# A half unit's split issued ahead of, instead of behind, each step of other work on ScalarE, VectorE and GpSimd

## The chip, the cores and the metric

The kernel runs on one core of a Trainium2 chip. The metric is the device time of one execution in microseconds (us). TensorE, VectorE, ScalarE and GpSimd appear in the profile as PE (weight loads apart as PEld), DVE, ACT and POOL; SyncE is SP.

## What is computed

The reference is a network of ten stages on one batch of 256 tokens of width 1024, all in float32. The first block has two layers. Layer 0 is a chunked gated linear attention with a small memory attention; layer 1 is a stick-breaking attention with the same kind of memory attention; each is followed by a PEER layer, which scores 2 x 128 keys for each of 8 heads, takes the best 16 of each side, then the best 16 of the 256 sums, and applies the chosen experts out of 16384:

```python
def peer(x, w_q, subkeys, u_tab, v_tab):
    ...
    s = jnp.einsum('nhpd,hpkd->nhpk', q, subkeys).astype(jnp.float32)
    top_s, top_i = lax.top_k(s, PEER_TOPK)
    ...
    best_s, best_pos = lax.top_k(cand_s, PEER_TOPK)
    idx = jnp.take_along_axis(cand_i, best_pos, axis=-1)
    g = jax.nn.softmax(best_s, axis=-1).astype(x.dtype)
    ...
        act = jax.nn.gelu(jnp.einsum('nd,nhkd->nhk', xt, u_tab[it]), approximate=False)
        return jnp.einsum('nhk,nhkd->nd', gt * act, v_tab[it])
```

The second block has two layers of feed-forward, mixer, feed-forward. The mixer joins four attentions (neighbourhood `na`, differential `df`, grouped `gq`, dilated `dl`) between one input and one output projection. All weights together are 933 units of 128 x 1024 numbers, and every unit is read once.

## The kernel before, in words

**Units and halves.** SP loads each unit (512 KB) into one of four buffers `RAW` (line 2542). A unit is used as two halves of 128 x 512. TensorE does not take float32 at full precision here: every weight half is split into a high part `WH` (ScalarE, `Scalar.split`, line 1026, the activation at line 1037) and a low part `WL` = `RAW` - `WH` (`Vector.split`, line 1573, at line 1580; for every fourth half of most stretches GpSimd instead, `Gpsimd.split`, line 2302, at line 2309; `low_on_pool` at line 32 says which). Both have `NHALF` = 5 slots. Each product is then three matmuls: high by high, high by low, low by high. All of TensorE's matmuls are recorded at line 415 and its transposes at line 419.

**What a split waits for.** `Scalar.split` of half j waits until its `RAW` has landed and until TensorE has used half j - 5, whose slot it takes over. The low split waits for the high one. TensorE waits, ahead of half j, for its low part. SP waits for both low parts of a unit before it loads the buffer again.

**The order of work.** The four engines run four programs that walk the same list of halves. TensorE does half j, then a `tick()`. On the other three, `halves(n)` does per half: a `tick()`, then the split of the half five ahead. At the start five halves are split, so when TensorE does half j, the other engines do `tick()` j and then the split of half j + 5. `Pace.tick` (line 99) advances every generator in `fg` by one step and those in `bg` by as many steps as the stage's `rate` gives credit for; each step yields its cost, the same number on each engine, so that step k of a generator lies at the same half on all four. The steps are the "other work": the attention of each kind (scores, turn, values), the norm and rotation of queries and keys (`norm`), the linear attention (`decay`, `inner`, `states`), the stick-breaking heads (`two_heads`), and in a PEER stage `route` and `gates`. Every engine takes its instructions in the order written.

**Around the ticks.** Work outside `tick()` stands between calls of `halves`: the copies out of PSUM after a group of halves, `gelu` on ScalarE after each pair of `u` units (line 1399), the split of the gate activations `GH` (ScalarE, line 1374) and `GL` (VectorE, line 2100) ahead of each `v` unit, and the norms between stages. At a stage's end four halves are held back and used together (`last_two`), and `next_stage` splits four halves with no tick between them.

**The PEER stage** (`peer_stage`: 851, 1376, 2102, 2431) has 32 halves of query projection; 128 halves of `u` with `route` in the background (rate 3.5, both blocks of 128 tokens, one after the other); 128 halves of `u` with `gates` part 0 (rate 0.55); then 256 halves of `v`, the first 128 of them with `gates` part 1. `route` on VectorE is a search for the top 16 (lines 1966 to 1987) and then a decode of wide operations (lines 2008 to 2046); GpSimd has two multiplications of it (line 2420). At its end TensorE transposes the result, for which it waits on the last of VectorE's reductions (line 2045). A step of `gates` is on VectorE either two comparisons (lines 2078, 2081) or three products and one multiplication out of PSUM (lines 2086, 2093), and in every second step TensorE does 24 small matmuls. In the first 128 halves of `v` GpSimd has no splits. For the `v` unit g TensorE waits for `GL` of g; there are two buffers of it, so `GL` of g + 1 is made while TensorE works on g.

**The stages without steps.** The feed-forward stages have no background work. Those with `which` = 1 have `mix_tables`: on ScalarE five loads at the first tick and one small exponential at the last, on GpSimd from the 13th tick some scalings and sums, on VectorE five small operations at the last.

Of the kernel before, what the change touches and what calls it, by code (L numbers as in the profile page):

```python
# [1017 lines left out]
class Scalar:  # L1018
# [20 lines left out]
    def halves(self, n):  # L1039
        for _ in range(n):  # L1040
            self.j += 1
            self.pace.tick()
            self.split()

    def start_load(self, name, dst, src):
        sem, n = self.c.load(name)
# [519 lines left out]
class Vector:  # L1566
# [14 lines left out]

    def halves(self, n):
        for _ in range(n):
            self.pace.tick()
            self.split()

    def own(self):

# [706 lines left out]
class Gpsimd:  # L2295
# [14 lines left out]

    def halves(self, n):
        for _ in range(n):
            self.pace.tick()
            self.split()

    def next_stage(self, stage):
        self.e.wait_ge(*self.c.xtl.at(stage + 1, 1, 1))
# [424 lines left out]
```

## Time and profile before

| | |
|---|---|
| median of 3 runs | 3193.7 us (3188.42 to 3195.05) |
| the profiled execution: its own time | 3195.57 us |
| its span in the trace | 3193.5 us |
| busy: PE, DVE, ACT, POOL | 95%, 66%, 50%, 15% |
| granted TensorE clock, mean | 0.974 |
| chain that ended last | PE 85%, DVE 10%, ACT 3%, issue 1%, DMA 1% |

The busy shares say which engine has work; the waits of PE, stage by stage, say what keeps it from working. A wait stands in brackets behind the instruction that ended it: `[2.60 <-DVE BIG L1767]` is 2.60 us in which the engine was idle, ended by VectorE's instruction at line 1767. The stages begin at about 75 (rest of the linear attention's projections), 174 (PEER), 1036 (stick-breaking), 1175 (PEER), 2042, 2244 (mixer), 2421, 2620, 2821 (mixer) and 2998 us of the span.

### The profile page before, as it was taken

Reading aid. Unit: us, or ns where it says so; the run is one execution under the profiler, and the core shown is the slowest. Engines: PE = TensorE matmul, PEld = TensorE weight load, DVE = VectorE, ACT = ScalarE, POOL = GpSimd, SP = SyncE. Lnnn points to the kernel's source line nnn. Section 1 sums busy time; section 2 is a strip of 40 time slices with the busy share of each in tenths; the row PEclk is TensorE's granted clock in tenths of the full one; section 3 lists DMA queues with packets and bytes.
Section 4 is the critical chain, followed back from the end, with each engine's and each line's share of the span. In section 5 each row is a group of like instructions: output and inputs, shape, how many; then the busy total and the mean of one; then the engine's idle time right before and its main releaser. Section 6 shows DMA issues by size and latency. Waiting matters only on the chain.

```text
span 3193.5 us, 56060 instructions
## 1 busy us (share of the span) xinstructions
PE 3029.3 (95%) x21820; PEld 2730.7 (86%) x21820; DVE 2097.6 (66%) x4342; ACT 1597.0 (50%) x3039; POOL 492.8 (15%) x371
## 2 busy tenths in 40 slices
PE   8989999999998989999999999799979999998899
PEld 8789999988787879999988888699768989976798
DVE  4559988799655456987879945654665455456544
ACT  5445544444555545554444455455535555553454
POOL 1213210000021112320000022222101213210121
PEclk9999999999999999999999999899989999999999
DMA  6345554444554334554445555455314556542354
GB/s 213 119 146 170 180 166 159 160 161 164 187 192 160 127 122 160 171 173 158 159 159 166 166 198 195 171 187 180 126 59 149 190 181 197 185 141 70 113 188 155
DMA packets 139512, 512.60 MB, mean 161 GB/s; under 512 B 15713, under 2 KB 16242, under 8 KB 137970
## 3 DMA queue, kind: packets, MB, share of 16 engines
q1 hardware_dynamic: 134352, 489.22, 46.6%
q10 hardware_dynamic: 4898, 19.81, 1.7%
q8 instruction: 174, 2.85, 0.4%
q14 instruction: 88, 0.72, 0.1%
HBM read 507.92 MB, written 1.05 MB: 159 GB/s over the span
## 4 chain that ended last, share of the span: by engine, by line
PE 85%; DVE 10%; ACT 3%; issue 1%; DMA 1%; ACTq 0%; DVEq 0%; SPq 0%
PE ps L415 84%; DVE WL L1580 2%; ACT WH L1037 1%; PE ps L419 1%; ACT BIG L1133 1%; DVE BIG L1692 1%; DVE BIG L1741 1%; DMA RAW<-in_w 0%; DVE XTl L1619 0%; DVE BIG L1655 0%; DVE H L1658 0%; DVE BIG L2025 0%; DVE BIG L1986 0%; DVE BIG L2032 0%; DVE BIG L1633 0%
## 5 line engine op out<-in xcount | busy, mean ns | idle before, releaser
L1037 ACT ACTIVATE WH<-RAW 128x512 fp32r<-128x512 f32 x1866 | 1168.5, 630 | 1193.8 <-PE ps L415 1167.1
L1580 DVE TENSOR_TENSOR WL<-RAW,WH 128x512 fp32r<-128x512 f32 x1537 | 1109.7, 725 | 868.6 <-ACT WH L1037 860.7
L415 PE MATMUL ps<-XTh,WH 128*128 128x256 f32 x3928 | 1131.6, 288 | 22.4 <-DVE XTl L1788 8.2
L415 PE MATMUL ps<-XTl,WH 128*128 128x256 f32 x3928 | 1120.6, 285 | 0.0
L415 PE MATMUL ps<-XTh,WL 128*128 128x256 f32 x3928 | 1119.9, 285 | 0.0
L2309 POOL TENSOR_TENSOR WL<-RAW,WH 128x512 fp32r<-128x512 f32 x329 | 441.3, 1341 | 2652.8 <-ACT WH L1037 2652.8
L415 PEld LDWEIGHTS ps<-XTh,WH 128*128 128x128 f32 x3928 | 762.9, 194 | 34.1 <-DVE WL L1580 14.5
L415 PEld LDWEIGHTS ps<-XTl,WH 128*128 128x128 f32 x3928 | 763.5, 194 | 3.1
L415 PEld LDWEIGHTS ps<-XTh,WL 128*128 128x128 f32 x3928 | 762.8, 194 | 0.0
L415 PE MATMUL ps<-WH,GH 128*128 128x512 f32 x1408 | 562.5, 399 | 20.0 <-DVE GL L2100 8.1
L415 PE MATMUL ps<-WL,GH 128*128 128x512 f32 x1408 | 554.0, 393 | 0.0
L415 PE MATMUL ps<-WH,GL 128*128 128x512 f32 x1408 | 553.2, 393 | 0.0
L415 PEld LDWEIGHTS ps<-WH,GH 128*128 128x128 f32 x1408 | 267.3, 190 | 78.1 <-issue 9.8
L415 PEld LDWEIGHTS ps<-WH,GL 128*128 128x128 f32 x1408 | 267.0, 190 | 57.8
L415 PEld LDWEIGHTS ps<-WL,GH 128*128 128x128 f32 x1408 | 267.6, 190 | 50.2
L415 PE MATMUL ps<-BIG 128*128 128x64 f32 (+6 forms) x966 | 154.2, 312 | 23.7 <-DVE BIG L1769 5.8
L415 PEld LDWEIGHTS ps<-BIG 128*128 128x128 f32 (+4 forms) x966 | 124.1, 190 | 48.5 <-issue 22.8
L415 PE MATMUL ps<-WH,XTh 128*128 128x512 f32 (+1 forms) x400 | 158.0, 395 | 4.4 <-DVE XTl L1619 1.3
L415 PE MATMUL ps<-WH,XTl 128*128 128x512 f32 (+1 forms) x400 | 150.1, 375 | 0.0
L415 PE MATMUL ps<-WL,XTh 128*128 128x512 f32 (+1 forms) x400 | 149.9, 375 | 0.0
L419 PE MATMUL ps<-CST,BIG 128*128 128x128 f32 x430 | 78.4, 322 | 61.7 <-DVE BIG L1692 36.6
L419 PEld LDWEIGHTS ps<-CST,BIG 128*128 128x128 f32 x430 | 59.8, 166 | 83.1 <-DVE BIG L1692 41.6
(182 smaller groups left out, 2209.3 us busy)
## 6 DMA issues: line engine op xcount, KB each, us to landing
RAW<-in_w SPq DMA_DIRECT2D x933, 512.0 KB, 3.3
BIG<-in_ln ACTq DMA_DIRECT2D x4, 1024.0 KB, 6.3
GAIN<-in_norms ACTq DMA_DIRECT2D x6, 512.0 KB, 4.1
BIG<-in_sk ACTq DMA_DIRECT2D x2, 1024.0 KB, 5.0
BIG<-in_na_bias ACTq DMA_DIRECT2D x2, 1024.0 KB, 10.2
BIG<-in_qk_gain ACTq DMA_DIRECT2D x2, 960.0 KB, 6.6
BIG<-in_memT ACTq DMA_DIRECT2D x4, 256.0 KB, 7.6
BIG<-in_xT ACTq DMA_DIRECT2D x1, 1024.0 KB, 5.5
```

What stands on the lines that cost most here:

```text
L415: return self.e.matmul(out, lhsT, rhs, start=start, stop=stop, skip_group_check=loose)
L419: return self.e.transpose(out, in_, self.c.IDENT[0:n, 0:n])
L1037: e.activation(wh, raw, ACT.Copy).then_inc(*c.hi.mark(j))
L1133: e.activation(t.E[:, i % 3, w], src[:, w], ACT.Exp, bias=s[:, blk:blk + 1], accum_out=s[:, 2 + blk:3 + blk]).then_inc(*c.exps.mark(tag, i ...
L1580: e.tensor_tensor(wl, raw, wh.bitcast(F32), ALU.subtract).then_inc(*c.lo_v.mark(j))
L1692: e.scalar_tensor_tensor(out=c.XN[:, blk, w], in0=c.H[:, blk, w], scalar=s[:, 3:4], in1=c.GAIN[:, w], op0=ALU.mult, op1=ALU.mult).then_inc ...
L1741: e.tensor_reduce(s[:, 0:2], src, AX, ALU.max, negate=True).then_inc(*c.maxed.mark(tag, i))
L2309: e.tensor_tensor(wl, raw, wh.bitcast(F32), ALU.subtract).then_inc(*c.lo_p.mark(j))
```

## The change

In the three programs that split, `halves` calls `self.split()` ahead of `self.pace.tick()`. The program of TensorE and that of SP are untouched, and so are `next_stage`, the start and all that stands between calls of `halves`. No instruction is added or removed.

```diff
@@ Scalar
     def halves(self, n):
         for _ in range(n):
             self.j += 1
+            self.split()
             self.pace.tick()
-            self.split()
@@ Vector
     def halves(self, n):
         for _ in range(n):
+            self.split()
             self.pace.tick()
-            self.split()
@@ Gpsimd
     def halves(self, n):
         for _ in range(n):
+            self.split()
             self.pace.tick()
-            self.split()
```

## Rows read from the trace of the kernel before

**Rows 1.** The page's first part: busy time, share of the span, instructions.

```profile
PE 3029.3 (95%) x21820; PEld 2730.7 (86%) x21820; DVE 2097.6 (66%) x4342; ACT 1597.0 (50%) x3039; POOL 492.8 (15%) x371
```

**Rows 2.** Waits of PE in the whole span: us in total, times, longest.

```profile
PE ps L415 <- DVE WL L1580: 8.0, 14, 2.5
PE ps L415 <- POOL WL L2309: 5.4, 2, 2.7
```

**Rows 3.** Groups by form: instruction xcount | busy, mean ns | idle before, releasers.

```profile
L1037 ACT ACTIVATE WH<-RAW 128x512 fp32r<-128x512 f32 x1866 | 1168.5, 630 | 1193.8 <-PE ps L415 1167.1 <-DMA RAW<-in_w 8.6 <-DVE XTl L1619 6.8
L1580 DVE TENSOR_TENSOR WL<-RAW,WH 128x512 fp32r<-128x512 f32 x1537 | 1109.7, 725 | 868.6 <-ACT WH L1037 860.7
```

**Rows 4.** Chain that ended last, behind the first route block: start, us, what.

```profile
322.88 59.04 PE ps L415 x492
```

**Rows 5.** Timeline of DVE in the first route block: start, us, instruction, idle before.

```profile
290.46 0.69 DVE L1580 TENSOR_TENSOR WL<-RAW,WH 128x512 fp32r<-128x512 f32 x1 [0.60 <-ACT WH L1037]
...
303.98 3.40 DVE L2032 TENSOR_TENSOR BIG<-BIG,CST 128x1024 f32<-128x1024 f32 x1
...
321.07 1.20 DVE L2045 TENSOR_REDUCE BIG<-BIG 128x64 f32<-128x1024 f32 x1
```

**Rows 6.** Timeline of POOL in the same block.

```profile
303.54 2.76 POOL L2420 TENSOR_TENSOR BIG<-BIG 128x1024 f32<-128x1024 f32 x1 [1.77 <-DVE BIG L2025]
306.26 3.94 POOL L2309 TENSOR_TENSOR WL<-RAW,WH 128x512 fp32r<-128x512 f32 x2
```

**Rows 7.** Timeline of PE in the same block: its two waits.

```profile
308.55 0.39 PE L415 MATMUL ps<-XTh,WH 128*128 128x256 f32 x1 [2.68 <-POOL WL L2309]
...
322.33 0.55 PE L419 MATMUL ps<-CST,BIG 128*128 128x128 f32 x3 [0.53 <-DVE BIG L2045]
```

**Rows 8.** Windows behind the first wait: PE, PEld, DVE, ACT, POOL busy, clock, DMA, GB/s.

```profile
309.80:313.10 3.30, 3.30 (x18) 3.30 (x17) 3.30 (x4) 0.66 (x2) 0.40 (x1) 0.50 0.49 158
```

**Rows 9.** Timeline of ACT among the first `v` units, with gates.

```profile
650.27 0.63 ACT L1037 ACTIVATE WH<-RAW 128x512 fp32r<-128x512 f32 x1 [0.79 <-PE ps L415]
```

**Rows 10.** Timeline of DVE there.

```profile
651.06 0.69 DVE L1580 TENSOR_TENSOR WL<-RAW,WH 128x512 fp32r<-128x512 f32 x1
651.66 0.42 DVE L2100 TENSOR_TENSOR GL<-BIG,GH 128x256 fp32r<-128x256 f32 x1
...
652.84 1.09 DVE L2086 TENSOR_TENSOR OHW<-ROWS,GT 128x512 bf16<-128x512 bf16 x3
653.85 0.68 DVE L2093 TENSOR_TENSOR BIG<-BIG,ps 128x512 f32<-128x512 f32 x1
```

**Rows 11.** Timeline of PE there: a half of six matmuls, then the gate matmuls.

```profile
651.37 0.39 PE L415 MATMUL ps<-WH,GH 128*128 128x512 f32 x1
...
652.73 0.90 PE L415 MATMUL ps<-ROWS,GAIN 128*128 128x64 bf16 x24
653.47 0.48 PE L415 MATMUL ps<-WH,GH 128*128 128x512 f32 x1
```

**Rows 12.** Timeline of ACT in the first mixer stage.

```profile
2327.82 0.63 ACT L1037 ACTIVATE WH<-RAW 128x512 fp32r<-128x512 f32 x1
```

**Rows 13.** Timeline of DVE there.

```profile
2328.48 0.69 DVE L1580 TENSOR_TENSOR WL<-RAW,WH 128x512 fp32r<-128x512 f32 x1 [1.07 <-ACT WH L1037]
2329.09 0.35 DVE L2171 TENSOR_TENSOR BIG<-BIG 128x192 f32<-128x192 f32 x1
```

**Rows 14.** Timeline of PE there, with the first and last such wait.

```profile
2271.42 1.14 PE L415 MATMUL ps<-BIG 64*128 64x256 f32 x8 [0.59 <-ACT BIG L1506]
...
2328.64 0.60 PE L419 MATMUL ps<-CST,BIG 128*128 128x128 f32 x4
...
2331.84 1.08 PE L415 MATMUL ps<-BIG 128*128 128x64 f32 x8 [2.60 <-DVE BIG L1767]
...
2396.42 1.08 PE L415 MATMUL ps<-BIG 128*128 128x64 f32 x8 [0.55 <-DVE BIG L1769]
```

**Rows 15.** Waits of PE from 1036 to 1175, the stick-breaking stage; columns as in rows 2.

```profile
PE ps L415 <- DVE BIG L1943: 2.0, 2, 1.2
```

## The prediction

> **What bounds the kernel now.** I read the page first, then PE's waits, the groups by form, the chain, and the timelines of five places. TensorE is busy 95% of the span [rows 1], so only what reaches its waits can move the time. A whole one: what is earlier or later on another engine, and is not waited for, is worth nothing. The splits are the largest work of ScalarE and VectorE, but both sit idle ahead of them: ScalarE 1167.1 us until TensorE has used a half, VectorE 860.7 us until ScalarE has the high part [rows 3]. TensorE waits the other way, for a low part, only 8.0 us in 14 times on VectorE and 5.4 us in 2 times on GpSimd [rows 2]: 13.4 us is all that an earlier split can give directly. The five halves of lead hide the rest.
>
> **What the change does to the order.** No instruction is added, so no duration changes by itself. On each engine the old order is step j - 1, split j + 4, step j, split j + 5; the new one is split j + 4, step j - 1, split j + 5, step j. Between two steps there stands one split, before and after. What differs is which: step j now stands behind split j + 5, which needs TensorE's half j to be done, where it stood behind split j + 4, which needed half j - 1. So a step that could begin while TensorE was in half j now waits for its end, then for ScalarE's split and, on VectorE, for its own. Only where a step of ScalarE is itself late, beyond the end of half j, is nothing lost. In return each low part is ready earlier by the step that stood before it.
>
> Moved with the steps are the five loads of `mix_tables` (ScalarE's queue, behind one split of 0.63 us; used twelve ticks later: nothing). SP's queue is not reordered; its waits are on low parts, which come no later relative to TensorE in the quiet stages, and earlier in the busy ones. In the projections of the feed-forward and in the last 128 halves of `v` the steps are empty: nothing.
>
> **Route, four blocks (two layers, two blocks of tokens).** Here both effects meet. In the decode, GpSimd multiplies from 303.54 for 2.76 us and only then does its split, from 306.26 [rows 6]; TensorE waits 2.68 us for that low part [rows 7], and behind the wait its clock is granted at 0.50 for 3.3 us [rows 8]: half of that, some 1.6 us, is lost as well. The new order does this split ahead of the multiplication, so both should go: 4.3 us a block, 17 in four. But VectorE has no gap between its split at 290.46 and the reduction at 321.07 over 0.2 us [rows 5], and TensorE, at 322.33, waits for that reduction, if only 0.53 us [rows 7]. VectorE sets when the block ends, so TensorE arrives earlier and waits there instead. And VectorE enters the full stretch later. At 290.46 it had finished its step and was idle 0.60 us [rows 5]; now it has the split first and the step behind it, so all later steps come one step and 0.6 us of idle time later. A step of the search is some 0.8 us: TensorE's half lasts 1.44 us (59.04 us for 492 matmuls, twelve to a half [rows 4]), less some 0.6 for the split. Together +1.4 us. The idle time of TensorE at the reduction becomes 0.5 + 4.3 + 1.4, some 6 us in one piece, and 2.68 us was enough to bring the clock down [rows 7, 8]; what it costs behind the reduction, 1.6 us, is not covered any more, as nothing follows on which TensorE would have waited. Bounds of a block: 0 (VectorE has reserves that I don't see) and +3.0. I take +2.0, nearer the upper one since the stretch is full. Four blocks: **+8**.
>
> The multiplication also holds up VectorE: L2032, begun 0.44 us after it, took 3.40 us [rows 5, 6]. "SBUF — State Buffer" of the Trainium skill (Who interferes with whom) says that an elementwise operation of VectorE with two inputs in SBUF and a GpSimd operation exclude each other, the later one blocked until the first is done; the row agrees. By that rule a GpSimd split moved ahead only changes which operation of VectorE stands still, and the sum stays.
>
> **First 128 halves of `v`, two stages.** GpSimd has no splits there and VectorE is nearly full. A half is 1.36 us and the gate matmuls add 0.74 [rows 11]. `GL` of the next unit must be there when TensorE ends its two halves. Old: at 650.27 ScalarE begins the split [rows 9], some 0.1 us after the half's end; VectorE's split follows at 651.06, `GL` at 651.66 [rows 10], 1.4 us after ScalarE's start. New: the step stands between split and `GL`. For the long kind it is 1.6 us (from 652.84 to 0.6 us behind 653.85 [rows 10]). From the half's end: 0.74 to the high part, 0.6 split, 1.6 step, 0.42 `GL` makes 3.36 us; TensorE needs it at 0.74 + 2 x 1.36 = 3.46. It fits by 0.1 us, and misses by about 0.1 where a short step ran just before. Taken: ten misses a stage, +1 us each stage. Bounds: 0, and +12 a stage if each of the 32 long steps costs a further 0.4 (the 0.42 of `GL` come free of cover). Two stages: **+2**.
>
> **Mixers, two stages.** Between 2271.42 and 2396.42 TensorE waits 17 times for steps, from 0.2 to 3.5 us; the first, one of the longest and the last have a row [rows 14]. In the wait at 2331.84 the chain is: ScalarE's split at 2327.82 [rows 12], VectorE's at 2328.48, its rotation from 2329.09 [rows 13], then L1767, then TensorE. In the new order this split is that of the half that TensorE ends at about 2328.6, where its transposes begin [rows 14]: ScalarE starts at about 2328.65 and not at 2327.82, so the wait is longer by 0.8 us. Where ScalarE was late itself, with exponentials beyond the half's end, it costs nothing. Bounds for a stage: 0, and 17 x 0.8 = 14. I take five of the 17, four microseconds, nearer the lower end since in most of them the attention's own chain goes on through the end of the half. Two stages: **+8**.
>
> **Stick-breaking.** Twelve heads, with TensorE waiting 2.0 us in 2 times for VectorE's mask [rows 15], so this chain has just run out of reserve; each of the six pairs can lose up to the 0.8 us of above. Bounds 0 and +5; taken **+3**.
>
> **Linear attention and start.** In the four `tokens` steps ScalarE's copy now stands behind a split of 0.63 us [rows 3], and the last of them leads into the next stage: +0.6. The steps of `decay`, `inner` and `states` are chains of several engines: bounds -1 and +4, taken +1.4. Together **+2**.
>
> **Sum:** 8 + 2 + 8 + 3 + 2 = +23 us on the profiled execution of 3195.57 us (span 3193.5), so 3218.6. That execution is 1.9 us above the median of the three, 3193.7; the forecast against the median is **3217 us**, 0.7% slower. What this measurement can tell from no change is about 0.2%, 6.4 us.
>
> A rule speaks against the change in one sentence: "ScalarE/VectorE/GpSimdE queues are strict FIFO" ("PSUM — Partial Sum Buffer" of the Trainium skill, Engine vs sequencer instructions). By it a waiting split holds all steps behind it; that VectorE's rotation starts at the end of the split, with 1.07 us idle before it [rows 13], agrees.
>
> **Rivals.** (a) *The starved splits were the cost* (faster). TensorE no longer waits in the decode, and VectorE ends the reduction early enough because the reordered GpSimd work holds it up less (3.40 us for one operation [rows 5] shows how much there is to win). It decides if VectorE reaches the reduction more than 0.5 us earlier than now. Then up to 4.3 us a block come back, -17, and with the mixers at 0 the time is 3177. For it: it is the only place with waits for low parts of over 2 us. Against: the unbroken row of work of VectorE. 0.12.
>
> (b) *Hidden.* Steps lose their head start, but PE's next demand lies two steps later almost everywhere; the mixers' chains are bound by ScalarE. Then 3194 to 3200. For it: 95% busy. Against: the wait at 2331.84. 0.12.
>
> (c) *`GL` becomes the bound* (slower by more). The 0.1 us of reserve above is not there; 12 us for each stage on top, and the upper halves of mixers and stick-breaking: 23 + 22 + 8 = +53, 3245. 0.14.
>
> That the change does nothing would need the waits of a split never to bite; it is in (b), since for the empty stages it is true.
>
> **How the numbers follow.** The forecast has 0.62; it lies over 6.4 us in 0.57 of it. Faster: 0.11 of (a). Same: 0.01 of (a), 0.12 of (b), 0.05 of the forecast: 0.18. Slower: 0.57 and the 0.14 of (c): 0.71. The range leaves out most of (a) and the upper half of (c): 3190 to 3242. Lower end: everything at its lower bound but a few us back in the decode; upper end: route 12, `v` 12, mixers 16, rest 9.
>
> **What would show it.** Right: no wait of PE on L2309 or L1580 over 1 us in the decode, and in their place one of 4 us or more on L2045 with a clock of 0.5 behind it; in the mixer the wait for L1767 at 3.4 us and not 2.60; the summed PE waits on L1767, L1142, L1736 and L1943 up; feed-forward stages as long as before to 0.5 us. Wrong: PE leaving L2045 earlier than 148 us into the PEER stage (322.33 less 174), or mixer stages shorter than the 177 us between 2244 and 2421; or waits on L2100 in the first half of `v`, which would be (c).

## The result, and the profile after

The changed kernel takes 3221.19 us (median of 6 runs, 3214.78 to 3226.52) against 3193.52 (6 runs of the kernel before beside it, 3188.42 to 3195.05): a ratio of 1.0089 [1.0076, 1.0102], slower by 27.7 us. The forecast was 3217 us, 23 slower. Sign, size and range held. Which stages the time comes from held only in part, and one of the forecast's reasons was wrong in sign.

The page of the kernel after, its first part and two groups by form, to be read against [rows 1, 3]:

```profile
PE 3044.0 (95%) x21820; PEld 2734.8 (85%) x21820; DVE 2098.5 (65%) x4342; ACT 1603.1 (50%) x3039; POOL 489.6 (15%) x371
...
L1037 ACT ACTIVATE WH<-RAW 128x512 fp32r<-128x512 f32 x1866 | 1170.4, 631 | 1285.4 <-PE ps L415 1254.1
...
L1580 DVE TENSOR_TENSOR WL<-RAW,WH 128x512 fp32r<-128x512 f32 x1537 | 1106.2, 723 | 944.5 <-ACT WH L1037 934.7
```

The same instructions on the other engines, as long as before. TensorE's own busy time grew by 14.7 us (3029.3 to 3044.0) for the same 21820 matmuls, with a mean granted clock of 0.971 and not 0.974: over half of the 26.9 us by which the span grew (3193.5 to 3220.4) is time in which TensorE was busy, not idle. What also grew is the standing in front of the instructions: 87 us more of ScalarE idle for TensorE's half (1167.1 to 1254.1), 74 us more of VectorE idle for the high part (860.7 to 934.7). The waits of TensorE in the kernel after (us in total, times, longest):

```profile
PE ps L415 <- DVE WL L1580: 16.1, 17, 3.3
PE ps L419 <- DVE BIG L1749: 9.2, 5, 2.2
PE ps L415 <- DVE GL L2100: 8.6, 6, 2.2
...
PE ps L419 <- DVE BIG L2045: 6.8, 4, 4.3
...
PE ps L415 <- DVE BIG L1943: 5.5, 5, 1.5
PE ps L419 <- ACT BIG L1142: 5.1, 6, 1.7
...
PE ps L415 <- DVE BIG L1767: 3.8, 2, 1.9
```

The same view of the kernel before, for the lines that changed most:

```profile
PE ps L419 <- ACT BIG L1142: 7.9, 8, 1.7
...
PE ps L415 <- DVE BIG L1767: 5.2, 2, 2.6
...
PE ps L419 <- DVE BIG L2045: 1.7, 2, 1.1
...
PE ps L419 <- DVE BIG L1749: 1.1, 2, 0.6
```

GpSimd's two waits [rows 2] are gone, and more has come in at VectorE's splits (8.0 to 16.1 us), at its copies of scores (1.1 to 9.2), at the end of `route` (1.7 to 6.8) and at the mask of stick-breaking (2.0 to 5.5). The waits on L1767 and L1142 went down.

**Where the time lies.** TensorE's matmuls come in the same order in every kernel here, so the k-th of one can be laid beside the k-th of another, and a stage is the time between two of them. This table is worked out that way from the profiled executions: the length before, and what each kernel adds to it. (The experiments are introduced below; x2 means both stages of that kind together.)

```
                          before |  after     e1     e4     e5     e7     e8    e10    e12
start                       64.6 |    1.1    0.1    1.9    0.5   -1.4    1.4   -0.3    0.0
linear attention            99.4 |    5.5    0.7    7.4    7.1    0.8    7.8   -0.1   -0.1
route, token block 0, x2   301.7 |    4.8    1.1    2.0    0.9   -1.4    7.9   -2.3    0.5
route, token block 1, x2   185.5 |    7.1    5.3    5.9    3.0    2.2    9.3    4.4    3.8
u with gates, x2           445.8 |   -1.3    0.8    1.7   -0.3    1.6   -1.3   -0.4   -1.2
v with gates, x2           419.2 |    5.4   -3.5   -1.7   -0.3   -3.5   -1.9   -5.2   -5.9
rest of v, x2              380.0 |    0.0    0.2    0.2    0.2    0.1    0.0   -0.1    5.9
stick-breaking             135.3 |    7.3   -1.6    1.4    2.7    0.1    3.6   -1.2   -1.1
first feed-forward         203.6 |   -3.1   -3.0   -2.7   -2.8   -2.9   -2.4    0.9    6.2
other feed-forward, x3     591.3 |   -2.1   -1.8    1.4    0.5   -1.9   -1.6    0.4   13.1
mixers, x2                 351.9 |    2.1  -25.8    2.1  -17.7   -4.9    1.3  -28.1  -18.4
sum                       3178.4 |   26.8  -27.3   19.5   -6.3  -11.2   24.1  -31.8    2.8
```

One execution each: e7 changes nothing but five loads and still shows -3.5 in `v` and -4.9 in the mixers. A cell under 3 to 5 us is not evidence by itself; one that comes back in several kernels with the same part is.

**Route.** The timeline of POOL in the first route block of the kernel after:

```profile
306.17 2.80 POOL L2420 TENSOR_TENSOR BIG<-BIG 128x1024 f32<-128x1024 f32 x1 [3.98 <-DVE BIG L2025]
308.92 1.75 POOL L2309 TENSOR_TENSOR WL<-RAW,WH 128x512 fp32r<-128x512 f32 x1
...
314.58 2.24 POOL L2309 TENSOR_TENSOR WL<-RAW,WH 128x512 fp32r<-128x512 f32 x1
```

The timeline of DVE there:

```profile
312.28 3.43 DVE L2032 TENSOR_TENSOR BIG<-BIG,CST 128x1024 f32<-128x1024 f32 x1
315.63 1.75 DVE L1580 TENSOR_TENSOR WL<-RAW,WH 128x512 fp32r<-128x512 f32 x1
...
328.30 1.21 DVE L2045 TENSOR_REDUCE BIG<-BIG 128x64 f32<-128x1024 f32 x1
```

The timeline of PE there, and its wait at the same point of the second PEER stage:

```profile
317.43 0.39 PE L415 MATMUL ps<-XTh,WH 128*128 128x256 f32 x1 [2.88 <-DVE WL L1580]
...
329.56 0.55 PE L419 MATMUL ps<-CST,BIG 128*128 128x128 f32 x3 [1.60 <-DVE BIG L2045]
...
1348.03 0.90 PE L419 MATMUL ps<-CST,BIG 128*128 128x128 f32 x3 [4.34 <-DVE BIG L2045]
```

The windows behind the first two of these waits (columns as in [rows 8]):

```profile
317.80:321.10 3.30, 3.30 (x20) 3.09 (x19) 3.30 (x5) 1.12 (x2) 0.00 (x0) 0.64 0.62 196
329.80:333.00 3.20, 3.20 (x29) 3.20 (x28) 2.43 (x8) 0.63 (x1) 0.17 (x1) 1.00 0.67 241
```

GpSimd's split is no longer late, and the starved split did not go away. It is now VectorE's: its split at 315.63 stands behind L2032, which took 3.43 us beside GpSimd's multiplication as it took 3.40 before [rows 5], and was then itself slowed to 1.75 us beside GpSimd's split. TensorE waits 2.88 us for it where it waited 2.68 [rows 7]. The whole piece of lateness moved from one engine's queue to the other's. At L2045 TensorE waits 1.60 us in this block and 4.34 in the same block of the second PEER stage.

The clock needs care. The wait of 2.88 us stands at the same matmul of the second PEER stage too (1333.89), and the one of 2.68 before [rows 7] at 1311.68. The windows just behind them, the first of the kernel after, the second of the kernel before:

```profile
1334.30:1337.60 3.30, 3.17 (x27) 2.99 (x27) 3.30 (x5) 1.28 (x3) 0.00 (x0) 1.00 0.71 207
1312.90:1316.20 3.30, 3.06 (x26) 2.85 (x25) 3.30 (x4) 1.26 (x2) 0.42 (x1) 1.00 0.46 155
```

The same wait, at the same place in the program, was followed by the half clock in one stage and by the full one in the other. Its length alone doesn't tell whether the clock falls.

**Mixer.** The place of [rows 12 to 14] in the kernel after, first the timeline of ACT:

```profile
2356.90 0.63 ACT L1037 ACTIVATE WH<-RAW 128x512 fp32r<-128x512 f32 x1
```

The timeline of DVE there:

```profile
2352.86 0.69 DVE L1580 TENSOR_TENSOR WL<-RAW,WH 128x512 fp32r<-128x512 f32 x1 [1.76 <-ACT WH L1037]
...
2355.21 0.68 DVE L1741 TENSOR_REDUCE BIG<-ps 128x2 f32<-128x512 f32 x1
...
2359.73 0.35 DVE L1767 SCALAR_TENSOR_TENSOR BIG<-BIG 128x128 f32<-128x128 f32 x1
```

The timeline of PE there:

```profile
2360.23 1.08 PE L415 MATMUL ps<-BIG 128*128 128x64 f32 x8 [1.92 <-DVE BIG L1767]
```

The wait was to become 3.4 us and is 1.92, below the 2.60 of before. VectorE still stands 1.76 us before its split at 2352.86, as at the same split before (2323.78, shown with e1 below).

### The profile page after: what moved, and what is told of

Read it like the earlier page. It is cut to its first block, busy times and chain, and to the rows that moved or that the text cites. A ratio compares the mean times of both kernels' runs of the same rounds, so it can differ in the third digit from the quotient of the medians.

```text
span 3220.4 us, 56060 instructions
## 1 busy us (share of the span) xinstructions
PE 3044.0 (95%) x21820; PEld 2734.8 (85%) x21820; DVE 2098.5 (65%) x4342; ACT 1603.1 (50%) x3039; POOL 489.6 (15%) x371
## 4 chain that ended last, share of the span: by engine, by line
PE 85%; DVE 10%; ACT 3%; issue 1%; DMA 0%; ACTq 0%; DVEq 0%; SPq 0%
PE ps L415 84%; DVE WL L1580 2%; ACT WH L1037 1%; PE ps L419 1%; DVE BIG L1692 1%; ACT BIG L1133 1%; DVE BIG L2032 0%; DVE BIG L1741 0%; DVE XTl L1619 0%; DVE BIG L2025 0%; DVE BIG L1655 0%; DVE H L1658 0%; DVE BIG L1633 0%; DVE BIG L1641 0%; DVE BIG L2045 0%
## 5 line engine op out<-in xcount | busy, mean ns | idle before, releaser
L1037 ACT ACTIVATE WH<-RAW 128x512 fp32r<-128x512 f32 x1866 | 1170.4, 631 | 1285.4 <-PE ps L415 1254.1
L1580 DVE TENSOR_TENSOR WL<-RAW,WH 128x512 fp32r<-128x512 f32 x1537 | 1106.2, 723 | 944.5 <-ACT WH L1037 934.7
L415 PE MATMUL ps<-XTh,WH 128*128 128x256 f32 x3928 | 1133.0, 288 | 25.7 <-DVE WL L1580 13.4
L2309 POOL TENSOR_TENSOR WL<-RAW,WH 128x512 fp32r<-128x512 f32 x329 | 438.1, 1332 | 2698.0 <-ACT WH L1037 2698.0
## 6 DMA issues: line engine op xcount, KB each, us to landing
BIG<-in_na_bias ACTq DMA_DIRECT2D x2, 1024.0 KB, 10.6
```

The source lines that it names most:

```text
L415: return self.e.matmul(out, lhsT, rhs, start=start, stop=stop, skip_group_check=loose)
L1037: e.activation(wh, raw, ACT.Copy).then_inc(*c.hi.mark(j))
L1580: e.tensor_tensor(wl, raw, wh.bitcast(F32), ALU.subtract).then_inc(*c.lo_v.mark(j))
L2309: e.tensor_tensor(wl, raw, wh.bitcast(F32), ALU.subtract).then_inc(*c.lo_p.mark(j))
```

## Experiments

All are full kernels that compute the same thing. The medians of the kernel before, measured beside them on the same chip, were 3193.24 us for e1 to e4 (13 runs), 3193.9 for e5 to e8 (19), 3192.17 for e9 and e10 (7) and 3192.6 for e11 and e12 (13).

### Which engine's order matters: e1_act, e2_act_dve, e3_pool

Of the change, e1 keeps ScalarE's part, e2 ScalarE's and VectorE's, e3 GpSimd's alone.

```diff
@@ Scalar (e1, e2) / Vector (e2) / Gpsimd (e3)
     def halves(self, n):
         for _ in range(n):
+            self.split()
             self.pace.tick()
-            self.split()
```

> Only ScalarE puts its split ahead of the step; VectorE and GpSimd keep the old order. Theory A (VectorE's steps lose their head start, because its split now waits for a half that TensorE is still in): VectorE's steps are not held up here, so the time stays within 5 us of the kernel before, 3189 to 3199. Rival B (ScalarE's own steps, exponentials and copies, come too late behind its split): most of the +28 us is here, over 3210. Rival C (the pair of both orders makes the loss, since each waits for the other): also near the kernel before, and e2_act_dve then has all of it.

> ScalarE and VectorE put the split first, GpSimd keeps the old order. Theory A: +24 to +30 us over the kernel before, since GpSimd's order is worth at most some us; in the decode of route TensorE's wait of 2.7 us for GpSimd's low part (L2309) stays. If GpSimd's order mattered (rival D: it holds up VectorE's two-input operations by its place) the time would be over 5 us from that of the changed kernel.

> Only GpSimd puts its split ahead of its step. Theory A: within 3 us of the kernel before; the wait of 2.7 us on L2309 in the decode goes, and TensorE waits the same time later, for L1580 or the reduction at L2045, since VectorE sets the end of the block. Rival (a) of the prediction (the starved splits were the cost): 8 to 17 us faster.

Measured: e1 3169.33 us, 0.9928 [0.9912, 0.9945]. e2 3220.88 us, 1.0089 [1.0073, 1.0106]. e3 3194.31 us, 1.0005 [0.9995, 1.0014].

GpSimd's order is worth nothing in total: e3 takes as long as the kernel before, and e2 as long as the kernel after. Inside, the waits do move. In e3 TensorE's waits on L2309 are gone, and two others have grown, as forecast for that run (8.0 and 1.7 us before):

```profile
PE ps L415 <- DVE WL L1580: 12.1, 20, 1.8
PE ps L419 <- DVE BIG L2045: 6.9, 4, 2.3
```

In e2 the waits on L2309, expected to stay at 2.7 us, are 10.6 us in 4, the longest 4.1. ScalarE's order alone makes the kernel 24 us *faster*, which none of the three theories had. VectorE's costs 52 us on top (3220.88 - 3169.33). The change is the sum of a gain and a loss twice as large, and a comparison of before with after shows neither.

The gain of e1 lies in one place of the table, the mixers: -12.9 us in each. The timeline of ACT in the first mixer of the kernel before, over one round of the attention:

```profile
2321.72 0.47 ACT L1133 ACTIVATE BIG<-ps,BIG 128x256 f32<-128x256 f32 x1 [2.29 <-DVE BIG L1741]
...
2323.11 0.64 ACT L1037 ACTIVATE WH<-RAW 128x512 fp32r<-128x512 f32 x1
2326.91 0.47 ACT L1133 ACTIVATE BIG<-ps,BIG 128x256 f32<-128x256 f32 x1 [3.16 <-DVE BIG L1741]
```

The timeline of DVE over the same round, before:

```profile
2320.95 0.68 DVE L1741 TENSOR_REDUCE BIG<-ps 128x2 f32<-128x512 f32 x1
...
2323.78 0.69 DVE L1580 TENSOR_TENSOR WL<-RAW,WH 128x512 fp32r<-128x512 f32 x1 [1.76 <-ACT WH L1037]
...
2326.13 0.68 DVE L1741 TENSOR_REDUCE BIG<-ps 128x2 f32<-128x512 f32 x1
```

VectorE's maximum (L1741) releases ScalarE's exponentials (L1133). Behind them in ScalarE's queue stands its split, behind that VectorE's split, behind that in VectorE's queue the next maximum, and that releases the next exponentials. A round from maximum to maximum takes 5.18 us, 1.76 of them VectorE standing before a split that TensorE needs only halves later. The two engines hand each other the turn through a piece of work that is not urgent. The same round on DVE in e1:

```profile
2317.83 0.68 DVE L1741 TENSOR_REDUCE BIG<-ps 128x2 f32<-128x512 f32 x1
...
2318.94 0.68 DVE L1580 TENSOR_TENSOR WL<-RAW,WH 128x512 fp32r<-128x512 f32 x1
...
2321.27 0.68 DVE L1741 TENSOR_REDUCE BIG<-ps 128x2 f32<-128x512 f32 x1
```

The high part was made before the exponentials, the split at 2318.94 has no wait, and the round is 3.44 us. The waits of DVE for the high part in the first mixer (2245 to 2420 us) of the kernel before:

```profile
DVE WL L1580 <- ACT WH L1037: 32.3, 27, 2.2
```

The same in e1 (2245 to 2407 us):

```profile
DVE WL L1580 <- ACT WH L1037: 14.9, 16, 2.0
```

And in the kernel after (2272 to 2448 us):

```profile
DVE WL L1580 <- ACT WH L1037: 43.3, 34, 2.6
```

TensorE gains by this in two ways. The windows of the same two stretches, before and in e1 (columns as in [rows 8]):

```profile
2245.00:2420.00 175.00, 149.86 (x765) 119.42 (x765) 106.81 (x229) 77.47 (x197) 18.64 (x14) 0.93 0.29 94
2245.00:2407.00 162.00, 143.26 (x763) 115.85 (x764) 106.92 (x228) 78.32 (x196) 18.93 (x14) 0.96 0.30 101
```

Of the 13 us, TensorE's idle time gives 6.4 (25.1 to 18.7) and its busy time 6.6, at a granted clock of 0.96 and not 0.93. Here the waits that went took some time at half clock with them.

With VectorE's order changed too, its split is one half further on and again stands before a high part that isn't there: 43.3 us. ScalarE's gain is given back almost to the microsecond (mixers -25.8 in e1, +2.1 after).

### The wait for the end of the half alone: e4_wait, e5_act_dvewait

These keep a split where it was and add to a step only what the change adds ahead of it: the wait until TensorE has used half j. e4 has it on ScalarE and VectorE in the old order; e5 is e1 with it on VectorE.

```diff
@@ Scalar.halves (e4) / Vector.halves (e4, e5)
         for _ in range(n):
+            self.e.wait_ge(*self.c.spent(self.made - NHALF))
             self.pace.tick()
             self.split()
```

> The old order, and ahead of each step ScalarE and VectorE also wait until TensorE has done the half that the step belongs to (the wait that the change puts there by way of the split), with no split moved. Theory A: this wait alone gives at least half of the loss, +14 to +25 us. Rival E (the place of a further split of 0.6 us, not the end of the half, is what costs): under +6 us.

> ScalarE puts its split first; VectorE keeps its order but waits, ahead of each step, until TensorE has done that step's half. It divides what VectorE's new order costs on top of ScalarE's (3169 without it, 3221 with it, 52 us) into the wait for the end of the half and the place of ScalarE's and VectorE's splits ahead of the step. If the lost head start is nearly all of it (as the prediction had it): 3205 to 3220. If the time that VectorE stands until ScalarE's split is done and its own has run is the larger part: 3175 to 3195.

Measured: e4 3212.1 us, 1.0058 [1.0041, 1.0074]. e5 3184.5 us, 0.9974 [0.9964, 0.9984].

The wait that the forecast costed is real: +19 us in e4, +15 on top of e1 in e5. Both fell where theory A (e4) and the second case (e5) had them. So of VectorE's 52 us, 15 are the wait for the end of the half and 36 are the split's place between the steps (3220.88 - 3184.5), if the two simply add up, which no run tries. The linear attention seems to show the wait most cleanly: +7.4 and +7.1 in e4 and e5, +5.5 after, +0.7 in e1 and -0.1 in e10, where it is absent. But e2, which is not in the table and has the wait on both engines, shows only +1.9 there. By the traces TensorE's idle time in the stage is 13.5 us before, 14.2 after, 15.3 in e2 and 17.8 and 17.5 in e4 and e5, at granted clocks of 0.95, 0.90, 0.96, 0.92 and 0.92: what the kernel after loses here is nearly all clock, which e2 doesn't lose, and in e4 and e5 about 4 of the 7 us are added idle time.

### Taking the gain without one suspected cost: e6_act_not_route, e8_v_old

e6 is e1 with ScalarE's old order in the halves that have `route`. e8 is the kernel after with VectorE's old order in the first 128 halves of `v`.

```diff
@@ Scalar.halves (e6, late = in the halves with route) / Vector.halves (e8, late = g < GP)
-            self.split()
-            self.pace.tick()
+            if self.late:
+                self.pace.tick()
+                self.split()
+            else:
+                self.split()
+                self.pace.tick()
```

> ScalarE puts its split first everywhere but in the 128 halves with route, where it keeps the old order; VectorE and GpSimd as before. In e1_act the route stretches were 6.5 us longer than before (0.5 and 3.0, 0.7 and 2.4 us). If this comes from ScalarE's split ahead of the exponential of route, on which VectorE waits: 3 to 6 us below e1_act, 3163 to 3167. If it is the run's own scatter: as e1_act, 3168 to 3171.

> The changed kernel, but VectorE has its old order in the first 128 halves of v of both PEER stages. If its steps between split and GL are what lengthened these stretches (3.3 and 2.1 us over before, 5.2 and 3.7 over e1_act): TensorE's waits on GL (L2100) fall from 8.6 to about 4 us and the time is 4 to 9 us under that of the changed kernel. If the lengthening comes from elsewhere: within 2 us of it.

Measured: e6 3171.8 us, 0.9931 [0.9914, 0.9947]. e8 3215.0 us, 1.0065 [1.0048, 1.0082].

e6 takes back e1's losses in the route stretches (+6.4 us there in e1, -1.0 in e6) and is no faster as a whole: the start and the first mixer were longer by about as much (5.0 us, and -6.3 us where e1 has -12.9). Whether that is scatter or a shift of phase stays open. e6 lies outside both ranges that were given for it. e8 is 6 us faster than the kernel after, by medians of different sessions (the intervals overlap a little: e8 up to 1.0082, the kernel after from 1.0076), and its `v` stages are 7.3 us shorter: VectorE's order very likely costs there. What I had expected of the waits on `GL` missed. They read 8.1 us in 4 in e8 and 8.6 in 6 after, so the cost of `v` is hardly in that wait.

### The loads: e7_loads_later

In the changed kernel the five loads of `mix_tables` also stand one split later. e7 is the kernel before with that alone.

```diff
@@ Scalar.mix_tables
+        yield
         self.start_load(f"qkg{layer}", ...)
...
-        for _ in range(12 + 4 + 8 + 1):
+        for _ in range(12 + 4 + 8):
             yield
```

> The kernel before, but ScalarE issues the five loads of mix_tables one half later (the only change in the first feed-forward stage, which was 3 us shorter in all kernels where ScalarE splits first or waits). If the place of the loads made that difference: the first feed-forward stage is 2 to 4 us shorter in the trace, a wait of TensorE for GL of 2.6 us behind the stage's start is gone, and the time is 1 to 5 us lower. If not, both stages are as before within 0.5 us.

Measured: 3186.99 us (10 runs), 0.9988 [0.9978, 0.9998]. The stage that I had costed at nothing is shorter by 2.9 us, as by 3.1 in the kernel after; the medians differ by 6.9 us and the ratio makes it 3.8, and what lies beyond the 2.9 is no more than the scatter of the stages. The view of DMA issues at the start of this stage (2040 to 2056 us) before, with KB each and the median us from issue to landing:

```profile
RAW<-in_w SPq DMA_DIRECT2D x4, 512.0 KB, 10.1
```

The same in e7 (2038 to 2052 us):

```profile
RAW<-in_w SPq DMA_DIRECT2D x4, 512.0 KB, 8.9
```

And from the timeline of PE before, its wait ahead of the first gate activations, which neither e7 nor the kernel after has:

```profile
2058.66 0.47 PE L415 MATMUL ps<-WH,GH 128*128 128x512 f32 x1 [2.56 <-DVE GL L2158]
```

The weights land 1.2 us earlier by the median of four, and the first of them far earlier: by its landing in the trace 10.3 us behind its issue before, 5.6 in e7. The table loads are not urgent, and two of them were issued ahead of that first weight; in e7 they come behind. ScalarE's split of it stands in its queue just ahead of the activation (L1455) that leads to the gate activations. That split in the timelines of ACT, before and in e7:

```profile
2054.69 0.63 ACT L1037 ACTIVATE WH<-RAW 128x512 fp32r<-128x512 f32 x1 [5.11 <-PE ps L415]
2048.96 0.63 ACT L1037 ACTIVATE WH<-RAW 128x512 fp32r<-128x512 f32 x1 [0.54 <-PE ps L415]
```

The view names PE as what ended the idle time, but before it was the unit's landing, at 2054.67, just ahead of the split; in e7 it landed at 2048.62. So here too a split for which TensorE does not wait stood ahead of a step for which it does, and the wait of 2.56 us is gone with it. That the table loads took the weights' place in the DMA engines fits these rows; no run tries it apart from the order of issue.

### Moving VectorE's split the other way: e9_act_lag, e10_lag, e12_lag2, e11_lag_loads

If a VectorE that stands before a high part is the cost, its split should come *later* than the step, by a whole half. With e10 VectorE makes the low part of half j + 4 where it made that of j + 5: one split fewer ahead of a stage, and the missing one at the stage's end.

```diff
@@ Vector
     def next_stage(self, stage):
-        for _ in range(4):
+        for _ in range(3):
             self.split()
...
     def deepnorm(self, stage, t, rms=False):
+        self.split()
...
     def add_to_h(self, stage, scale):
+        self.split()
...
-        self.split()
         self.halves(12)
```

e9 is the same with ScalarE's split first as in e1, e12 is two splits behind (old order on ScalarE), e11 is e10 with e7's loads.

> ScalarE splits first; VectorE keeps the old order and is one split behind (the low part of half j + 4 behind step j; it catches up at each stage's end). With e1_act (half j + 5 between steps j and j + 1) and e2_act_dve (half j + 6) it is the third point of one line: the same instructions in the same order, only the half that VectorE's split between two steps belongs to differs. If what costs is that VectorE stands at a split whose high part does not exist yet, holding the next step: VectorE's idle time on L1037 in a mixer falls below e1_act's 14.9 us and the time is 0 to 10 us under e1_act, 3159 to 3170. If the shorter lead of the low parts weighs more: route and the first v stretch longer, over 3173.

> The kernel before with VectorE one split behind as in e9_act_lag; ScalarE unchanged. In the old order VectorE's split of half j + 5 waits for ScalarE's, which stands behind ScalarE's step j, which itself waits for VectorE's maximum and the like. If this chain from engine to engine is what e1_act removed (mixers 12.9 us shorter each), it goes here too without touching ScalarE: mixers 8 to 14 us shorter each, 3168 to 3180. If e1_act won by something else (ScalarE's high parts or loads earlier): 3188 to 3197.

> e10_lag, and ScalarE issues the five loads of mix_tables one half later, as in e7_loads_later (first feed-forward stage 3.0 us shorter there). In e10_lag that stage was 0.9 us longer than before. If the loads are what its low parts' lead was spent on: 2 to 5 us under e10_lag, 3159 to 3163. If the lag already costs at that stage's start for another reason: within 1.5 us of e10_lag.

> VectorE two splits behind (half j + 3 behind step j), ScalarE as before. If the gain of the lag is that VectorE no longer stands at splits without a high part, there is little left to win (7.9 us of idle time on L1037 in a mixer with the lag of one), and the lead of low parts is down to three halves, some 4.2 us: TensorE's waits on L1580 grow in route, where VectorE is full: 3165 to 3185, slower than e10_lag. If a shorter lead is simply better for VectorE's steps: 3150 to 3163.

Measured: e9 3168.3 us, 0.9921 [0.9904, 0.9937]. e10 3164.49 us, 0.9913 [0.9897, 0.993]. e11 3161.66 us, 0.9904 [0.9888, 0.9921]. e12 3195.99 us, 1.0014 [1.0002, 1.0025].

e10 changes nothing on ScalarE and gains 28 us; the mixers alone show -28.1. The same round of the attention in e10, with two lines added ahead of these in its file (L1743 is L1741):

```profile
2313.74 0.68 DVE L1743 TENSOR_REDUCE BIG<-ps 128x2 f32<-128x512 f32 x1
...
2314.74 0.68 DVE L1580 TENSOR_TENSOR WL<-RAW,WH 128x512 fp32r<-128x512 f32 x1
...
2317.08 0.68 DVE L1743 TENSOR_REDUCE BIG<-ps 128x2 f32<-128x512 f32 x1
```

No wait, and 3.34 us for a round. With e1 the exponentials moved behind ScalarE's split; with e10 VectorE asks for a high part one older. Both cut the same link, and doing both (e9) adds nothing. (In a mixer e9 and e10 have 7.8 and 7.9 us of such waits, e1 14.9, as e9's forecast said.) Waits of DVE for the high part in the whole span, in e10:

```profile
DVE WL L1580 <- ACT WH L1037: 392.8, 422, 6.3
```

against 860.7 us [rows 3] and 934.7 after. The price of the lag is reserve. Waits of TensorE for VectorE's low parts in e10:

```profile
PE ps L415 <- DVE WL L1580: 22.1, 23, 3.9
```

The same in e12:

```profile
PE ps L415 <- DVE WL L1580: 45.0, 33, 5.1
```

One half of lag adds 14 us of such waits (8.0 before, [rows 2]), and the kernel is still 28 us faster; two add 37, the feed-forward stages and the last of `v` grow by 25 us (table), and nothing is won. That is slower than the 3165 to 3185 that I expected, and route, where I looked for the loss, has only 4.3 of it. So there is a best place. VectorE's split between steps j and j + 1 belongs to half j + 3 in e12 (3196 us), j + 4 in e9 and e10 (3168, 3164), j + 5 in e1 and before (3169 and 3193), j + 6 in the change (3221).

e11 is the fastest kernel of the study, 31 us faster than before and 60 faster than the changed one. That the loads are what makes it better than e10 is not shown: 2.8 us is within the scatter, and its first feed-forward stage is 1.4 us longer than before, as in e10 (0.9) and not shorter as in e7.

## Why the prediction was right and wrong

The total was close, +23 forecast and +27.7 measured, partly because two errors cancelled: in the mixers neither the gain of 26 us nor the loss of 28 was forecast, and that their sum came near the forecast is luck.

**"13.4 us is all that an earlier split can give directly"** was the step that failed. It counts TensorE's waits for low parts and so sees what an earlier split gives to TensorE. A high part that is earlier also frees VectorE, which stands before it 860.7 us in the kernel before [rows 3]. I read that number as idle time that costs nothing, since VectorE is not the bound. But VectorE's steps are queued behind it, and in the mixer they are what TensorE waits for. The forecast said of ScalarE's part only that in some places "nothing lost"; the run has it as a gain of 24 us.

**Mixers, +8:** measured +2.1, made of -25.8 for ScalarE (e1) and +28 for VectorE. The estimate took one wait (2.60 us) to 3.4 by adding 0.8 to the start of ScalarE's split. In the trace that wait is 1.92: two rotation steps ran back to back with no split of VectorE between them, and the time is lost in other rounds: the waits on VectorE's copies of scores (L1749) are 1.2 us in the two mixers before and 8.6 after. The waits on L1767, L1142, L1736 and L1943 together, forecast to rise, went from 16.6 to 15.9 us, and only the last of them rose. Neither price nor mechanism held; that the two stages moved little was the outcome of a balance that I did not see.

**Route, +8:** +11.9 (4.8 and 7.1), in e1 already +6.4. By blocks the kernel after has +0.6, +3.1, +4.2 and +4.0 where each was to be +2.0. One reading was wrong from the start: 4.3 us of GpSimd's late split were counted in each of four blocks, 17 us in all, while [rows 2] has that wait two times. It stands in the first block of each stage (308.55 and 1311.68); in the second blocks TensorE waited 2.45 us for a split of VectorE (401.63 and 1404.76), which the forecast did not treat. And behind the wait at 1311.68 the clock stood at 1.00, so the half clock was not a price of each block either. Right: VectorE sets the end of the block, and GpSimd's earlier split does not help; PE leaves L2045 148.8 us into the first stage (329.56 less 180.76) against 148.2 before. Wrong: "no wait on L1580 over 1 us in the decode" (2.88 us), and the 4 us at L2045 with half clock came in one block of the four (4.34 us, with transposes of 0.90 us behind it where the first block's take 0.55). In the first block the wait was 1.60 and the clock stood at 1.00 behind it. That GpSimd's split only changes which operation of VectorE stands still, with the same sum, came out: taken as time over the median of the same instruction, VectorE's operations beside a working GpSimd lost 35.5 us in the four blocks before and 33.8 after.

**First half of `v`, +2:** +5.4 in the table. e8 undoes VectorE's part and is 6 us faster. The term was too small, and not by the sharp failure of rival (c), for the waits on `GL` rose only from 8.1 to 8.6 us.

**Stick-breaking, +3:** +7.3, with the mask's waits up from 2.0 us in 2 [rows 15] to 5.5 in 5. The mechanism is the forecast's; with e2, the same kernel but for GpSimd, at +2.5, its size isn't known to better than some 5 us.

**Linear attention and start, +2:** +6.6. That the steps "are chains of several engines" was said, and priced at 1.4; e4 and e5 show 7 us in the linear attention for the wait for the half's end alone, e2 with the same wait only 1.9, and the clock makes most of that difference.

**Feed-forward, "as long as before":** -5.2, of which -3.1 is the first stage. "The loads: nothing" was wrong by that: the queue that I priced was ScalarE's, and what mattered was what the loads did to the weights' landing.

**The rivals.** (a) is refuted: earlier low parts of GpSimd are worth nothing (e3). (b) held for the last of `v` (0.0) and for GpSimd. (c) did not come (its sum of +53 would also be 3247 and not 3245). That a waiting split holds all steps behind it was the right thing to weigh, and I applied it to one engine at a time. Applied to the loop of two queues, it would have given the gain as well.

**Open:** route's second blocks are some 2 us longer each even in e10. There VectorE's operations beside a working GpSimd are 15 in a block and lose 14.3 us, where before they were 7 and lost 8.5: with the lag its splits fall beside GpSimd's. That is read from the traces and no run tries it; in e1, where the two blocks are as much longer, only 8 operations and 9.9 us are so. Open is also how the stages before shift those behind them by 2 to 6 us (e6, e7).

## What to carry to other kernels

Where two in-order engines hand work back and forth, look for a non-urgent item of one engine's queue on which the other's urgent work stands: idle time "waiting for the high part" is then a cost even on an engine that is a third idle. Decouple it by letting the consumer lag one item behind the producer (28 us here, for four changed lines), and no further than the buffers' reserve allows. When a change reorders several engines at once, measure each one alone: here a gain of 24 and a loss of 52 were one edit.

## What the runs showed that I had not expected

- A wait of 1.60 us was followed by a granted clock of 1.00 (329.80 to 333.00), one of 2.88 us by 0.64 (317.80 to 321.10), one of 2.68 by 0.50 [rows 7, 8]. But the same two waits one PEER stage later, 2.88 and 2.68 us, were followed by 1.00. The half clock is no fixed price of a wait of that length.
- About half of what the mixers gained in e1 is not idle time but TensorE's matmuls at a higher granted clock (0.93 to 0.96).
- Beside a GpSimd operation different two-input operations of VectorE were held up, as they came: L2032 took 3.43 us, and a split 1.75 where it takes 0.69 elsewhere. Once it went the other way: in the kernel before an L2032 began at 397.61, 0.15 us ahead of GpSimd's multiplication; it took 1.21 us, and the multiplication 3.27 where it takes 2.80 at 392.10.
- Where five loads are issued, without any of them being waited for, was worth 3 us in a stage of 204.
